# Two narrow matmuls or one wide one: joining the high and low activations in three residual projections

## What is computed

```
h = h + swiglu(rmsnorm(h, norm_ffn[i]), ffn_w_in[i], ffn_w_out[i])        # second of two
return (jax.nn.silu(gate) * up) @ w_out                                   # D_FF = 2816
...
h = h + sqrelu_mlp(rmsnorm_2(h, mlp_norm[l]), w_up[l], w_down[l])         # both
return jnp.square(jax.nn.relu(x @ w_up)) @ w_down                         # D_FF_2 = 4096
```

## Time and profile before

| | |
|---|---|
| median of three runs | 1182.88 us |
| span of the profiled execution | 1182.2 us |
| TensorE busy | 1169.6 us (99%), 9738 matmuls |
| VectorE busy | 819.2 us (69%) |
| ScalarE busy | 691.5 us (58%) |
| GpSimd busy | 89.5 us (8%) |
| mean granted TensorE clock | 0.998 |
| ffn1_out, mlp0_out, mlp1_out | about 60, 87 and 87 us |

### The profile page before, as it was taken

One profiled execution on the slowest core, in us unless ns is written; L12 is line 12 of the kernel. 1 busy time (PEld: TensorE's weight loads), 2 busy tenths in 40 slices (PEclk: granted clock), 3 DMA queues, 4 the chain that ended last, 5 costly groups with the idle time before them and its releaser, 6 DMA issues. The chain is left out here.

```text
span 1182.2 us, 25988 instructions
## 1 busy us (share of the span) xinstructions
PE 1169.6 (99%) x9738; PEld 1140.9 (97%) x9738; DVE 819.2 (69%) x1296; ACT 691.5 (58%) x1115; POOL 89.5 (8%) x97
## 2 busy tenths in 40 slices
PE   8999999999999999999999999999999999999998
PEld 8999999999998899999999989999999979999998
DVE  7767866665577877666668997675567677776543
ACT  6635765654455567666556976664447576666432
POOL 1000200000110020000120000000013223000000
PEclk9999999999999999999999999999999999999999
DMA  7532655555664336555664556666666424566663
GB/s 270 177 94 89 193 178 177 177 178 192 200 202 144 107 107 190 191 190 193 209 209 155 193 180 192 191 193 191 206 212 205 142 77 153 185 193 193 202 195 106
DMA packets 57577, 207.84 MB, mean 176 GB/s; under 512 B 6352, under 2 KB 7568, under 8 KB 57248
## 3 DMA queue, kind: packets, MB, share of 16 engines
q1 hardware_dynamic: 57136, 203.52, 54.6%
q0 software_dynamic: 288, 3.21, 0.7%
q10 hardware_dynamic: 80, 0.07, 0.0%
HBM read 205.66 MB, written 1.05 MB: 175 GB/s over the span
## 5 line engine op out<-in xcount | busy, mean ns | idle before, releaser
L1679 DVE TENSOR_TENSOR w_lo<-w_raw,w_hi 128x1024 fp32r<-128x1024 f32 x379 | 463.4, 1225 | 68.7 <-ACT w_hi L511 68.1
L511 ACT CAST w_hi<-w_raw 128x1024 fp32r<-128x1024 f32 x379 | 395.1, 1045 | 174.1 <-PE acc L1006 172.2
L1004 PE MATMUL acc<-x_hi,w_hi 128*128 128x256 f32 (+1 forms) x1688 | 479.0, 284 | 2.2 <-DVE w_lo L1679 1.5
L1005 PE MATMUL acc<-x_lo,w_hi 128*128 128x256 f32 (+1 forms) x1688 | 473.3, 280 | 0.0
L1006 PE MATMUL acc<-x_hi,w_lo 128*128 128x256 f32 (+1 forms) x1688 | 473.2, 280 | 0.0
L1004 PEld LDWEIGHTS acc<-x_hi,w_hi 128*128 128x128 f32 x1688 | 317.8, 188 | 6.0 <-DVE x_lo L1699 1.8
L1005 PEld LDWEIGHTS acc<-x_lo,w_hi 128*128 128x128 f32 x1688 | 317.7, 188 | 0.5
L1006 PEld LDWEIGHTS acc<-x_hi,w_lo 128*128 128x128 f32 x1688 | 317.6, 188 | 0.0
L1004 PE MATMUL acc<-m_hi,w_hi 128*128 128x256 f32 x512 | 141.3, 276 | 0.0
L1005 PE MATMUL acc<-m_lo,w_hi 128*128 128x256 f32 x512 | 141.3, 276 | 0.0
L1006 PE MATMUL acc<-m_hi,w_lo 128*128 128x256 f32 x512 | 141.3, 276 | 0.0
(11 more groups left out here) (370 smaller groups left out, 1671.3 us busy)
## 6 DMA issues: line engine op xcount, KB each, us to landing
w_raw<-weights SPq DMA_DIRECT2D x381, 512.0 KB, 4.0
bias<-bias_rows POOLq DMA_DIRECT2D x1, 2048.0 KB, 8.7
h<-hT SPq DMA_DIRECT2D x4, 272.0 KB, 4.5
bias<-bias_rows POOLq DMA_DIRECT2D x1, 1088.0 KB, 8.9
outT<-h SPq DMA_DIRECT2D x4, 256.0 KB, 4.6
con<-constants SPq DMA_DIRECT2D x1, 913.0 KB, 9.3
w_raw<-weights SPq DMA_DIRECT2D x2, 256.0 KB, 3.1
par<-cols SPq DMA_DIRECT2D x1, 84.0 KB, 2.0
```

The lines of the kernel that those rows point to most:

```text
L511: nc.scalar.copy(w_hi[:, slot, :], w_raw[:, slot, :]).then_inc(hi_ready, 1)
L1004: nc.tensor.matmul(out, wh, xh[:, k, tok], start=first and n == 0, stop=False)
L1005: nc.tensor.matmul(out, wh, xl[:, k, tok], start=False, stop=False)
L1679: V.tensor_tensor(w_lo[:, slot, :], w_raw[:, slot, :], w_hi[:, slot, :].bitcast(F32), ALU.subtract)\
```

## The change

In ffn1_out, mlp0_out and mlp1_out, for output tiles 0 to 6 of 8, the first two matmuls of each weight tile become one. The high and low activations lie in one tensor `[P, 2, tiles, columns]`, and one matmul streams the 256 columns of both against the high weight tile, into all 512 columns of the bank. The third matmul (low weight, high activation) adds to the first 256 columns. So the bank holds two halves, and VectorE adds both to h, the second half first, with a wait for its own end between the two adds. The eighth output tile is computed as before. ffn0_out, with 272 columns, is left as it is.

```diff
+class Part:
+    def __init__(self, tile, part):
+        self.tile, self.part = tile, part
+    def __getitem__(self, key):
+        p, n, cols = key
+        return self.tile[p, self.part, n, cols]
+class Split:
+    def __init__(self, tile):
+        self.hi, self.lo, self.pair = Part(tile, 0), Part(tile, 1), Part(tile, slice(0, 2))
...
-        mid_hi = get("mid_hi", [P, 24, ROW], F32R)
-        mid_lo = get("mid_lo", [P, 24, ROW], F32R)
+        mid = Split(get("mid", [P, 2, 24, ROW], F32R))
+        mid_hi, mid_lo = mid.hi, mid.lo
...
-        m_hi = get("m_hi", [P, FF2T, SEQ], F32R)
-        m_lo = get("m_lo", [P, FF2T, SEQ], F32R)
+        m_both = Split(get("m", [P, 2, FF2T, SEQ], F32R))
+        m_hi, m_lo = m_both.hi, m_both.lo
...
                     k = k0 + n
+                    if both is not None:
+                        nc.tensor.matmul(out.rearrange("p (b t) -> p b t", b=2), wh, both.pair[:, k, tok],
+                                         start=first and n == 0, stop=False)
+                        ins = nc.tensor.matmul(out[:, 0:SEQ], wl, both.hi[:, k, tok], start=False,
+                                               stop=last and n == ntiles - 1)
+                        continue
...
-                        unit(u, b % RING, acc[j][:, 0:n], xh, xl, tok, c == 0, c == kunits - 1,
-                             ktail if c == kunits - 1 else TILES, TILES * c, gate if j == 0 else None)
+                        wide = both if both is not None and m != mt + KD - 1 else None
+                        unit(u, b % RING, acc[j][:, 0:2 * SEQ if wide else n], xh, xl, tok, c == 0, c == kunits - 1,
+                             ktail if c == kunits - 1 else TILES, TILES * c, gate if j == 0 else None, wide)
...
-                         (s_("mid_lo_ready"), FFT * layer))
+                         (s_("mid_lo_ready"), FFT * layer), mid if layer else None)
...
-                residual(f"mlp{layer}_out", m_hi, m_lo, st, 4, TILES, (s_("m_ready"), FF2T * layer))
+                residual(f"mlp{layer}_out", m_hi, m_lo, st, 4, TILES, (s_("m_ready"), FF2T * layer), m_both)
...
                     unit_done(phase, kunits * n + kunits - 1)
+                    if halves and n < KD - 1:
+                        own_wait(dve, V.tensor_tensor(h[:, n, tok], h[:, n, tok], acc[n % 4][:, SEQ:2 * SEQ], ALU.add))
                     V.tensor_tensor(h[:, n, tok], h[:, n, tok], acc[n % 4][:, 0:n_tok], ALU.add).then_inc(acc_free, 1)
...
                 unit_done("mlp1_out", 4 * n + 3)
+                if n < KD - 1:
+                    own_wait(dve, V.tensor_tensor(h[:, n, xt], h[:, n, xt], acc[n % 4][:, SEQ:2 * SEQ], ALU.add))
                 last = V.tensor_tensor(h[:, n, xt], h[:, n, xt], acc[n % 4][:, 0:SEQ], ALU.add).then_inc(acc_free, 1)
```

More of the change, by code:

```diff
@@ L994, in _, with unit @@
         def _(pe):
-            def unit(u, slot, out, xh, xl, tok, first, last, ntiles=TILES, k0=0, gate=None):
+            def unit(u, slot, out, xh, xl, tok, first, last, ntiles=TILES, k0=0, gate=None, both=None):
                 pe.wait_ge(lo_ready, u + 1)
@@ L1007, in unit, with four @@
                 return ins.then_inc(units_used, 1)
-            def four(phase, k, mt, stride, i, xh, xl, tok, gate=None, kunits=1, ktail=TILES, norm=None, norm_at=0):
+            def four(phase, k, mt, stride, i, xh, xl, tok, gate=None, kunits=1, ktail=TILES, norm=None, norm_at=0,
+                     both=None):
                 n = tok.stop - tok.start
@@ L1035, in sum_squares, with residual @@
                     .then_inc(stat_ready, 1)
-            def residual(phase, xh, xl, tok, kunits, ktail, gate):
+            def residual(phase, xh, xl, tok, kunits, ktail, gate, both=None):
                 for i in range(2):
-                    four(phase, 0, MT[phase], 4 * kunits, i, xh, xl, tok, gate, kunits, ktail)
+                    four(phase, 0, MT[phase], 4 * kunits, i, xh, xl, tok, gate, kunits, ktail, both=both)
             allt, xt = slice(0, T), slice(META, T)
@@ L1706, in inverse, with residual @@
                 dve.wait_ge(rstd_ready, NORM[norm] + 1)
-            def residual(phase, kunits, gain, norm, tok, hi=x_hi, lo=x_lo):
+            def residual(phase, kunits, gain, norm, tok, hi=x_hi, lo=x_lo, halves=False):
                 n_tok = tok.stop - tok.start
@@ L1936, in gated_mlp @@
                 else:
-                    residual("ffn1_out", 3, "final_a", "lru", tok, xs_hi, xs_lo)
+                    residual("ffn1_out", 3, "final_a", "lru", tok, xs_hi, xs_lo, True)
             gated_mlp(0, allt)
@@ L2318, in _ @@
             relu_mlp(0, "mlp0")
-            residual("mlp0_out", 4, "kv_norm", "att2", xt, xs_hi, xs_lo)
+            residual("mlp0_out", 4, "kv_norm", "att2", xt, xs_hi, xs_lo, True)
             ahead("k2", 0)
```

## The result

The changed kernel took 1191.86 us (median of four runs, 1190.85 to 1193.38) against 1182.73 us (four runs, 1182.33 to 1183.76): ratio 1.0077, 95% interval 1.0064 to 1.009. It is 9.1 us slower. The forecast was 1182.0 us, its range ended at 1186.8, so the result lies outside.

What follows compares the result with a forecast made beforehand. TensorE, busy 99% of 1182.2 us, was taken as the bound; 602 joined matmuls saving 1.5 ns each gave -0.9 us, adds and seams 0. That made 1181.3 us of span, 1182.0 us with 0.7 carried over; range 1177.8 to 1186.8.

Steps and rivals of the forecast that it cites:

- X: Start-to-start distance of a 512-column matmul on TensorE in the three stages, taken as 225.2 ns against 226.7 for two narrow.
- the adds are hidden: VectorE's 21 more adds, 0.46 us per tile, 9.7 us in all, claimed to be off TensorE's path.
- the seams: Where TensorE runs into new inputs after each residual, 2.6 us; claimed to cost what they cost now: 0.
- Step (a): 512-column matmuls of the same format in the first attention's value expansion: 232.1 ns each, 5.4 dearer than two of 113.3.
- Step (b): Second attention's value product: w_hi at 117.5 ns per 256 columns, two are 235.0; wide form saves 2.9, giving 223.8 ns.
- (c): From 272 columns at 123.3 ns: time strictly proportional to columns, so 226.7 ns for 512 and the change gives nothing.
- rival 2: Wide matmuls on TensorE cost 232.1 ns wherever they stand: +3.3 us, 1186.2 us; chance 0.28.
- its compounding: Wide matmuls also push the following narrow one from 113.3 to 117.5 ns: 9.6 ns a weight tile, +5.8 us, 1188.7.
- the eighth tile costs what it costs now: In each stage the last output tile keeps three narrow matmuls and its single add, so its seam and tail add 0.
- Rival 1: The weight load paces narrow TensorE matmuls, so 512 columns take 216 to 220 ns: gain 4.0 to 6.4 us; chance 0.27.
- The lower end (d): Plain f32 matmuls of 256 columns, 216 ns apart, read as 512 columns' work at the fastest: -6.4 us.

Runs made afterwards that it cites:

- the kernel with narrow halves: Against the changed kernel, the wide matmul is written as two matmuls of 256 columns, the 21 extra adds kept: 1183.73 us against 1184.06, ratio 1.0.

## Why the prediction was wrong

**What held.** That TensorE alone counts, that the price of the form is X times 602, that the adds are hidden (shown by the kernel with narrow halves: ratio 1.0), 0.46 us for each, the seams as before, no new wait of TensorE for w_lo, and the weight loads off the path. VectorE is busy 8.2 us longer (about 9 forecast).

**The step that failed is the choice of X.** Step (a) had the right row: 232.1 ns for the same form. Step (b) took from it that against its own neighbours the wide form saved 2.9 ns, and (c) that time is strictly proportional; both were put above the direct measurement, and X was set at 225.2. Measured: 235.0. The comparison of (b) was invalid because the 117.5 of the earlier trace rows and the 113.3 of the earlier trace rows are two rhythms, not two prices of two streams. The trace of before had this already: the first unit of the same value product, with the same w_hi streamed, runs at 113.4 ns (23 distances in 2.61 us), and only the later units, from which the earlier trace rows come, at 117.5 to 118:

```profile
930.62 0.28 PE L1533 MATMUL acc<-w_hi,x_hi 128*128 128x256 f32 x1
...
933.23 0.28 PE L1535 MATMUL acc<-w_lo,x_hi 128*128 128x256 f32 x1
```

The wide form does not inherit the quick one at this place. Against two narrow matmuls that is 602 x (235.0 - 226.7) = 5.0 us instead of -0.9.

**Second, that neighbours keep their distance.** The narrow matmul behind went from 113.3 to 118.3: 602 x 5.0 = 3.0 us. The prediction had this only in rival 2, as a possible 117.5. And "the eighth tile costs what it costs now" failed by 86 x 13.3 ns = 1.1 us. Together 5.0 + 3.0 + 1.1 = 9.1 us.

**The rivals.** Rival 2 named the mechanism, the place and the side (5.8 us with its compounding, chance 0.28); it was short because X lay 2.9 ns above the row that it used, the neighbour 0.8 above, and the eighth tile was missing. It should have been the likeliest case, and the range should have taken in its compounding, which had been left out on purpose. Rival 1 fell: the load is a floor of 112 ns up to 224 columns and gives nothing back at 512. The lower end (d), 216 ns, belonged to another number format and no 512-column matmuls of this one came near it (226.1 on the mean at the least, the first of two in a row). The isolated warm gap that the Trainium skill gives (TensorE: Matmul & The Clock Gate, section Back-to-back issue gap), N/2.4 + 2.5 ns, would put 512 columns at 215.8 ns, an estimate from that page; the trace has 235.0, and the measurement decides.

**What stays open.** That place and history choose the rhythm is shown; why the engine has two rhythms is not. That the load of the next weight tile meets the stream of this one would fit that the relative place counts and that with 16 stationary columns no distance at 256 columns reaches 113.3. It was argued and not isolated, and two results do not follow from it: the same relative place modulo 128 gave 120.0 ns with the activations moved and 118.7 with the weights moved, and a short load on one matmul of a turn left the turn at 346.7 ns or more.

## What to carry to other kernels

Price a matmul by start-to-start distances of the same form in its own trace, and where such a row exists, take it over any correction from another form. Before matmuls are joined to save their number, ask what the narrow one costs over its columns: here 113.3 ns for 256 columns was already below the stream's own 0.447 ns a column, so there was nothing to save and a rhythm to lose. When a layout changes, compare distances in untouched stages too: 64 bytes of padding moved this kernel by 9 us (the MLP activations) and by 30 (the weights).

## What the runs showed of the hardware that was not expected

- The place of the moving run relative to the weight tile changes the distance of 256-column matmuls. Modulo 128 bytes: 113.3 ns at 64 bytes apart, 118.3 at 32, and at the same place 120.0 with the activations moved and 118.7 with the weights moved. Moving the weight buffers and h cost 30 us (1213.24 against 1183.6, one run each).
- For the wide matmul of two runs it is the place of the second run that counts: a turn takes 346.7 ns with it 64 bytes on and 353.3 without, whichever of the two places the first has.
- Identical matmuls ran at 113.3 or 117.8 ns for as long as their group lasted, by what had run before; a mix of two narrow per wide was followed by the first, a turn of wide and narrow at this place or one 64-column matmul by the second; a plain f32 matmul behind the second brought back the first in two cases of three.
- A 256-column matmul with 128 stationary columns (113.3) can be quicker than with 16 (116.7 to 117.6), though it has the longer load.
